# The residual adds of a two-layer transformer kernel, moved from VectorE to GpSimd's line of loads and stores

## What is computed

```python
# first layer (RMS norm before the residual add)
x = x + rms_norm(merged @ w_o, norm_mix_post)              # phase D
h = rms_norm(x, norm_ffn_pre)
f = (silu(h @ w_ffn_gate) * (h @ w_ffn_up)) @ w_ffn_down
x = x + rms_norm(f, norm_ffn_post)                          # phase E
# second layer (no norm on the branch)
h = x + mix @ w_out                                         # phase G
h = h + conv_ffn(rmsnorm(h, norm_ffn_g), ...)               # phase H
return rmsnorm(h, norm_final_g)
```

## Time and profile before

| | |
|---|---|
| median of 3 runs | 3463.88 us (3463.38 to 3464.99) |
| time of the profiled execution | 3461.77 us |
| its span | 3460.1 us |
| TensorE matmul busy | 3073.1 us (89%) |
| VectorE busy | 1639.6 us (47%) |
| ScalarE busy | 1067.8 us (31%) |
| GpSimd busy | 359.4 us (10%) |

### The profile page before, as it was taken

The page is one execution under the profiler, slowest core; times in us unless marked ns, Lnnn a source line. Parts: engine busy times, 40 slices in busy tenths (PEclk is TensorE's granted clock), DMA queues, the critical chain, the costliest instruction groups (busy, mean ns, idle before and its releaser), DMA issues.

```text
span 3460.1 us, 38038 instructions
## 1 busy us (share of the span) xinstructions
PE 3073.1 (89%) x15115; PEld 2516.4 (73%) x15115; DVE 1639.6 (47%) x2080; ACT 1067.8 (31%) x1537; POOL 359.4 (10%) x363
## 2 busy tenths in 40 slices
PE   4889899999889769999999958898768899999997
PEld 3667778777767658888888846776556688888885
DVE  3355474574674363333333362443443554544545
ACT  3441441532623341111111133444443312222222
POOL 0110110210221100000000011332330000000000
PEclk8999999999989879999999978998789899999998
DMA  2321222212222432111111123323224211111112
GB/s 87 86 87 46 76 83 62 75 61 74 87 86 105 163 122 86 61 42 42 57 46 37 48 91 107 92 82 112 94 104 158 79 37 42 61 42 42 61 42 91
DMA packets 218370, 264.29 MB, mean 76 GB/s; under 512 B 10606, under 2 KB 174716, under 8 KB 218252
## 3 DMA queue, kind: packets, MB, share of 16 engines
q1 hardware_dynamic: 195040, 185.64, 16.8%
q0 software_dynamic: 12320, 43.82, 3.8%
q10 hardware_dynamic: 10892, 33.21, 3.3%
HBM read 200.72 MB, written 61.92 MB: 76 GB/s over the span
## 4 chain that ended last, share of the span: by engine, by line
PE 78%; DVE 9%; ACT 4%; DMA 4%; issue 3%; ACTq 1%; POOL 1%; SPq 0%; DVEq 0%
PE PS L322 28%; PE PS L596 19%; PE PS L345 18%; PE PS L1363 2%; DVE h_gained L402 1%; PE PS L1329 1%; PE PS L1267 1%; PE PS L2347 1%; PE PS L2336 1%; PE PS L1256 1%; DMA sb_branch<-u_scratch 1%; ACT hH L411 1%; DVE hL L416 1%; ACTq L474 1%; PE PS L2378 1%
## 5 line engine op out<-in xcount | busy, mean ns | idle before, releaser
L596 PE MATMUL PS<-hH,w_H 128*128 128x512 f32 x1072 | 456.5, 426 | 15.8 <-DVE w_L L307 8.0
L322 PE MATMUL PS<-hH,w_H 128*128 128x512 f32 x1408 | 436.3, 391 | 15.3 <-DVE hL L416 15.3
L322 PE MATMUL PS<-hL,w_H 128*128 128x512 f32 x1408 | 434.9, 390 | 0.0
L322 PE MATMUL PS<-hH,w_L 128*128 128x512 f32 x1408 | 434.6, 390 | 0.0
L596 PE MATMUL PS<-hH,w_L 128*128 128x512 f32 x1072 | 429.9, 401 | 0.0
L596 PE MATMUL PS<-hL,w_H 128*128 128x512 f32 x1072 | 428.6, 400 | 0.0
L307 DVE TENSOR_TENSOR w_L<-w_raw,w_H 128x1024 fp32r<-128x1024 f32 x192 | 238.0, 1241 | 325.8 <-ACT w_H L302 324.2
L1859 DVE TENSOR_TENSOR ffn_sum<-ffn_sum,PS 128x1024 f32<-128x1024 f32 x176 | 214.7, 1220 | 300.2 <-PE PS L345 300.2
L322 PEld LDWEIGHTS PS<-hH,w_H 128*128 128x128 f32 x1408 | 264.4, 188 | 72.6 <-DVE hL L416 16.1
L322 PEld LDWEIGHTS PS<-hL,w_H 128*128 128x128 f32 x1408 | 265.3, 188 | 55.5
L322 PEld LDWEIGHTS PS<-hH,w_L 128*128 128x128 f32 x1408 | 265.1, 188 | 55.4
(11 more groups left out here) (365 smaller groups left out, 4484.0 us busy)
## 6 DMA issues: line engine op xcount, KB each, us to landing
w_raw<-in_w_in SPq DMA_DIRECT2D x63, 512.0 KB, 4.2
u_scratch<-unit_staged SPq DMA_DIRECT2D x50, 512.5 KB, 4.4
w_raw<-in_w_up SPq DMA_DIRECT2D x44, 512.0 KB, 3.9
w_raw<-in_w_ffn_gate SPq DMA_DIRECT2D x22, 512.0 KB, 3.8
w_raw<-in_w_ffn_up SPq DMA_DIRECT2D x22, 512.0 KB, 3.8
down_raw<-in_w_ffn_down SPq DMA_DIRECT2D x11, 1024.0 KB, 4.9
down_raw<-in_w_down SPq DMA_DIRECT2D x11, 1024.0 KB, 5.0
u_scratch<-unit_staged_f SPq DMA_DIRECT2D x21, 512.0 KB, 4.2
```

What stands on the lines that cost most here:

```text
L322: mm = e.matmul(PS[:, bank + half, :], w[:, k, :], x[:, k - x0, half * HALF:(half + 1) * HALF], start=(i == 0 and j == 0), stop=(i == len( ...
L596: mm = e.matmul(PS[:, half, :], w[:, k0 + k, :], x[:, k, half * HALF:(half + 1) * HALF], start=(k == 0 and j == 0), stop=(k == nk - 1 and ...
```

## The change

The add of `x_res` leaves `dve_x` and stands, with the same waits, in `res_dma`, ahead of each block's store and load. In H GpSimd waits for the block's sum itself (`block_summed`), in G for ScalarE's copy, in D and E for VectorE's product with the gain. Nothing else is changed; the lines behind move by 16, 17 or 8.

```diff
--- before.py
+++ after.py
@@ -1589,6 +1589,22 @@
 
 
 
+        def x_add(e, tag, b, bufs, stored):
+
+            y, xr, x1 = (yacc if tag in "EH" else bufs[3])[:, b, :], bufs[1][b % 2], bufs[2][b % 2]
+            if tag in "DE":
+                e.wait_ge(sem("y_gained"), since(tag, "y_gained", b + 1))
+            elif tag == "G":
+                e.wait_ge(sem("y_copied"), since(tag, "y_copied", b + 1))
+            else:
+                block_summed(e, tag, b)
+            e.wait_ge(sem(f"x_loaded{b % 2}"), since(tag, f"x_loaded{b % 2}", 16 * (b // 2 + 1)))
+            if b >= 2:
+                if stored:
+                    e.wait_ge(sem(f"x_stored{b % 2}"), since(tag, f"x_stored{b % 2}", 16 * (b // 2)))
+                e.wait_ge(sem("block_normalised"), since(tag, "block_normalised", b - 1))
+            e.tensor_tensor(x1[:, :], y, xr[:, :], ALU.add).then_inc(sem("x_new"), 1)
+
         def res_dma(e, tag, src, dst, bufs, gain=None):
 
             if gain is not None:
@@ -1596,6 +1612,7 @@
             for b in range(2):
                 e.dma_start(bufs[1][b][:, :], src[:, b, :]).then_inc(sem(f"x_loaded{b}"), 16)
             for b in range(NB):
+                x_add(e, tag, b, bufs, dst is not None)
                 e.wait_ge(sem("x_new"), since(tag, "x_new", b + 1))
                 if dst is not None:
                     e.dma_start(dst[:, b, :], bufs[2][b % 2][:, :]).then_inc(sem(f"x_stored{b % 2}"), 16)
@@ -1656,7 +1673,7 @@
                 .then_inc(sem("std2"), 1)
 
         def dve_x(e, tag, b, bufs, yacc_, y_norm, stored=True):
-            y, xr, x1 = y_of(bufs, b, yacc_), bufs[1][b % 2], bufs[2][b % 2]
+            y = y_of(bufs, b, yacc_)
             if yacc_ is not None:
                 block_summed(e, tag, b)
             if y_norm:
@@ -1667,15 +1684,6 @@
                 e.wait_ge(sem("rstd"), since(tag, "rstd", b + 1))
                 e.scalar_tensor_tensor(out=y, in0=y, scalar=rstd[:, b:b + 1], in1=bufs[5][:, :],
                                        op0=ALU.mult, op1=ALU.mult).then_inc(sem("y_gained"), 1)
-                e.wait_ge(sem("y_gained"), since(tag, "y_gained", b + 1))
-            elif yacc_ is None:
-                e.wait_ge(sem("y_copied"), since(tag, "y_copied", b + 1))
-            e.wait_ge(sem(f"x_loaded{b % 2}"), since(tag, f"x_loaded{b % 2}", 16 * (b // 2 + 1)))
-            if b >= 2:
-                if stored:
-                    e.wait_ge(sem(f"x_stored{b % 2}"), since(tag, f"x_stored{b % 2}", 16 * (b // 2)))
-                e.wait_ge(sem("block_normalised"), since(tag, "block_normalised", b - 1))
-            e.tensor_tensor(x1[:, :], y, xr[:, :], ALU.add).then_inc(sem("x_new"), 1)
 
         def dve_h(e, tag, b, bufs):
             e.wait_ge(sem("std2"), since(tag, "std2", b + 1))
```

## The result

The changed kernel takes 3478.63 us (median of 5 runs, 3477.91 to 3482.49) against 3463.88 us before (median of 5 runs on the same chip, 3458.01 to 3465.18), a ratio of 1.0048 with a 95% interval of 1.0033 to 1.0062. It is 14.8 us slower. The forecast was 3479 us.

The account below looks back on a forecast made before the run. VectorE's line was taken to bound the ends of D and E, with GpSimd and VectorE excluding each other. Terms 6.4 + 3.9 + 2.1 + 2.7 + 0.5 = 15.6 on 3461.8, plus 2.1 to the median: 3479 us, range 3461 to 3485.

Parts of the forecast that it names:

- two near ties in B: Profiled starts of VectorE and GpSimd: VectorE went first when 0.04 us ahead, GpSimd when 0.07 us ahead.
- silent stretch: Start differences between -0.04 and +0.07 us, where the trace shows no winner; GpSimd's add was put 0.03 us ahead.
- the first rival: D and E: VectorE's scaling goes first, E -6.6, D's second half +1.0, sum +0.9, 3465 us; chance 0.28.
- E, +6.4 us: End of E: the add holds VectorE's scaling; blocks 2 to 7 cost 5.5 us more, the two before 1.0.
- D, second half, +3.9 us: D, blocks 4 to 7: adds hold product and scaling; L402 comes 2.1 us later, blocks 6 and 7 cost 0.91 each.
- D, first half, +2.1 us: D, blocks 0 to 3: `w_L` stands behind the held scaling, so TensorE goes on at 1225.95 instead of 1223.83.
- the fourth case: Slower still: GpSimd first, late loads in G and H, perhaps TensorE's lower clock in D; +22, 3486 us; chance 0.14.
- G, +2.7 us: End of G: slower adds delay block 7's load, issued 7.2 us behind add 4's start; last scaling 2682.2 against 2679.60.
- H, +0.5 us: H: engines alternate at 3.57 us a block, loads allow 7.1 us for two; +0.5 us, from -0.4 to +4.7.
- a sign of being wrong: In H: adds that wait for their loads in the next profile would show the prediction wrong.
- the likeliest case: GpSimd's add goes first in the tie and VectorE's scaling is held: 3479 us, 3474 to 3484; chance 0.50.
- one hand-over decides 17 us: Closing claim: the sum fails wherever the tie in D and E falls otherwise, since one hand-over decides 17 us of it.

Follow-up runs that it names:

- e1: Changed kernel, but in D and E GpSimd's add also waits for VectorE's small reciprocal, so that the scaling starts first; 3463.92 us, ratio 1.0000 to before.
- e3: Changed kernel with VectorE's gain (L402) of one block put ahead of the next block's reciprocal and scaling in E; 3467.04 us, ratio 1.0010 to before.
- e8: Kernel before, all adds on VectorE, plus an addition on GpSimd in E's blocks 0 to 6 that nobody reads; 3474.28 us, ratio 1.0036.
- e6: Kernel before with GpSimd adds only in E and D's blocks 4 to 7, and the gain ahead of the scaling there; 3454.77 us, ratio 0.9975.

## Why the prediction was right

**The lock and the tie.** The step on which most of the sum hung was the reading of two near ties in B. They left a silent stretch between 0.04 us for VectorE and 0.07 us for GpSimd, and I put 0.03 us on GpSimd's side, with 0.50 against 0.28. It was 0.01 to 0.02 us, and GpSimd went first in all twelve blocks of D and E in which the two met so closely. e1 moved that start by 0.12 us, and E moved by as much as the first rival had said (-7.0 for -6.6). In D's second half e1 isn't that rival (-2.2 for +1.0): its wait also keeps the add of block 5 0.10 us behind the start of the scaling of block 4, where the rival had the add go first. The Trainium skill, "SBUF — State Buffer", section "SBUF: two separate sides", has the rule (an exclusive lock, kept by the one that starts first for its whole instruction). The traces of after, e1, e3 and e8 agree with it: 2.87 against 0.75 us for the scaling behind the add, 2.89 against 2.34 for the add behind the scaling. The Trainium skill also says there that only an operation of VectorE with two SBUF inputs or in a 2-port mode is held; L402, with its large input in PSUM, kept 1.22 us beside the add in e1 and e3. The scaling reads one SBUF tensor and was held nevertheless; by that rule of the Trainium skill it is an operation in a 2-port mode, and no run here shows the mode itself.

**E, +6.4 us.** Measured +6.1: a block of 8.98 us for 9.03. GpSimd needed 0.30 + 0.58 + 0.53 us between adds (1.41 us) for the 1.51 assumed.

**D, second half, +3.9 us.** Measured +3.7: L402 came 7.96 us after block 4's product (7.96 = 1265.53 - 1257.57) for the predicted 8.08.

**D, first half, +2.1 us.** This term was mis-sized. The wait for `w_L` was worked out right, 2.60 us, and it is worth 2.1 (e3). The other 1.5 us are TensorE's lower clock behind it, which I had put into the fourth case and not into the sum. The later splits cost nothing, as assumed (D1 in e3 is the wait alone).

**G, +2.7 us.** Measured +2.6 by its parts: the load of block 7 was issued 7.05 us behind add 4 (7.2), add 7 started 5.2 us later (5.0 and 0.08), L402 4.7 us after that. (The parts in the prediction give 2682.17 - 2679.60 = 2.6, not 2.7.) Four executions have this code in G, and they cost 2.3 to 2.8 us.

**H, +0.5 us.** Measured +1.2, within its bounds. The loads took a median of 4.7 us for the 4.4 assumed, and from the third block on every add waited for its load, by 0.42 to 1.40 us. The prediction had named that as a sign of being wrong, and this one sign did come: its 7.1 us for two blocks was 7.6 in the last six ((3466.25 - 3447.27) / 5 = 3.80 a block). By its own rate (1.8 us for a landing 0.6 us later) 0.3 us more would cost 0.9. Its upper end of 4.7 for a landing of 5.5 doesn't follow from that rate, which gives 3.3 on top of the 0.5. The four executions with this code in H cost 0.8 to 2.1 us.

So the mechanism was the likeliest case with two pieces of the fourth, the clock in D and the late loads in H. That one hand-over decides 17 us doesn't come out of the prediction's own sums, which differ by 14.7 (15.6 and 0.9); the medians of after and e1 differ by 14.7 too.

The terms came to 15.6 us predicted and 17.2 measured; the difference is about the clock in D, as the other terms missed by +0.7 and -0.6 together. The stretches outside them took back 0.3 us (17.2 to 16.9 between the spans, 3460.1 and 3476.9), and the medians stand 14.8 us apart, 2 us less than these two executions. That 3479 and 3478.63 agree within 0.4 us is therefore luck: the forecast's terms were 1.6 us short, and it added 2.1 us because the profiled execution before lay that far below its median, while the one after is its own median. The runs of one kernel spread over 5 to 15 us.

## What to carry to other kernels

Before work moves from VectorE to GpSimd, look at what VectorE does in the same microseconds: if it reads SBUF the way the moved work does, the two take turns, and the moved work takes twice as long (2.34 us for 1.22). Here that was a loss of 14.8 us on an engine that is 10% busy where the moved work went first, and no change where it went second (e1). Put it beside what reads PSUM or beside a wait, as in e6 (3.9 us by the stretches, not separated by the medians), and keep it away from places where another engine's operand stands in the same line (`w_L` in D). When two instructions of a repeated block start within some hundredths of a microsecond of each other, work out both outcomes and try the one that one wait more decides.

## What the runs showed beyond that

- A start 0.02 us earlier was enough to hold the other engine out for 2.3 us, block after block; for VectorE 0.11 us (e1, 2031.04 against 2031.15) and 0.06 us (e8, 2039.46 against 2039.52) were enough.
- A wait of TensorE of the same length in the same code was followed by 1.2 GHz in one kernel (2.60 us, after) and by full clock in another (2.62 us, e3). Such a wait can have two prices, here 2.1 and 3.6 us for D's first half, each from one execution.
- On GpSimd, adding a 128x1024 tensor to itself took about 1.83 us once it could start (an estimate from e8: 2039.52 + 2.92 - 2040.61), adding two different ones 2.33.
